# Moving twenty modulation tiles into the attention of a one-core diffusion step, with its cached keys, biases and rope prepared earlier

## The reference, cut to what matters

```python
def adaln(cond, w, b):
    m = jax.nn.silu(cond) @ w + b                 # w: 2048 x 12288, one for each of the two layers
    return [t[:, None, :] for t in jnp.split(m, 6, axis=-1)]

def att_mixer_lat(h, w_in, w_out, sink, rpb, ak, av, bk, bv):
    qa, ka, va, qb, kb, vb = att_project(h, w_in)  # w_in: 2048 x 4608
    qb, kb = rope_2d(qb), rope_2d(kb)
    oa = neighbourhood_attention(qa, ka, va, ak, av, rpb)        # 8 heads, bias rpb, cached keys ak
    ob = window_attention(qb, kb, vb, bk, bv, sink)              # 8 query heads, 2 key heads, cached keys bk
    return jnp.concatenate([oa, ob], axis=-1) @ w_out            # w_out: 2048 x 2048
```

## Time and profile before

| what | value |
|---|---|
| median of 3 runs | 2515.88 us (2503.49 to 2517.59) |
| the profiled execution's own time | 2511.74 us, its span 2509.9 us |
| TensorE busy | 2355.8 us, 94% of the span |
| VectorE, ScalarE busy | 1485.8 us (59%), 1106.8 us (44%) |
| DMA | 593.13 MB, 236 GB/s over the span |
| mean granted TensorE clock | 0.975 |

### The profile page before, as it was taken

The page is one execution under the profiler, slowest core; times in us unless marked ns, Lnnn a source line. Parts: engine busy times, 40 slices in busy tenths (PEclk is TensorE's granted clock), DMA queues, the critical chain, the costliest instruction groups (busy, mean ns, idle before and its releaser), DMA issues.

```text
span 2509.9 us, 29857 instructions
## 1 busy us (share of the span) xinstructions
PE 2355.8 (94%) x12307; PEld 1837.7 (73%) x12307; DVE 1485.8 (59%) x2049; ACT 1106.8 (44%) x1529; POOL 83.9 (3%) x139
## 2 busy tenths in 40 slices
PE   5999968879999999999997999898999999999996
PEld 3766666558888887877776777666888888778775
DVE  3464663255545455766766768764656556666665
ACT  2332242233333334555553358733444444555553
POOL 1000000000000000000000001000000000000000
PEclk9999989989999999999998999998999999999998
DMA  8898926966777777676674877777455655766763
GB/s 296 303 322 312 333 101 216 337 219 210 251 251 250 246 251 260 219 256 220 204 253 170 303 274 250 260 268 256 152 186 186 199 185 184 257 218 220 243 224 110
DMA packets 296407, 593.13 MB, mean 236 GB/s; under 512 B 11568, under 2 KB 11824, under 8 KB 296016
## 3 DMA queue, kind: packets, MB, share of 16 engines
q1 hardware_dynamic: 289744, 574.77, 66.0%
q0 software_dynamic: 6528, 16.46, 2.0%
HBM read 587.76 MB, written 3.42 MB: 236 GB/s over the span
## 4 chain that ended last, share of the span: by engine, by line
PE 82%; DMA 7%; DVE 6%; ACT 3%; issue 1%; POOL 0%; SPq 0%; DVEq 0%; ACTq 0%; POOLq 0%
PE bank L583 22%; PE bank L573 14%; PE bank L575 13%; PE bank L574 13%; PE bank L585 11%; PE bank L541 5%; DMA raw<-in_w_att_in 3%; DVE w_lo L1103 2%; DMA raw<-in_w_att_out 2%; DMA raw<-in_w_rec_in 1%; PE bank L689 1%; ACT w_hi L827 1%; PE bank L600 1%; DMA raw<-in_w_ada 1%; PE bank L558 1%
## 5 line engine op out<-in xcount | busy, mean ns | idle before, releaser
L1103 DVE TENSOR_TENSOR w_lo<-raw,w_hi 128x1024 fp32r<-128x1024 f32 x712 | 857.6, 1221 | 553.4 <-ACT w_hi L827 551.6
L827 ACT ACTIVATE w_hi<-raw 128x1024 fp32r<-128x1024 f32 x712 | 733.5, 1050 | 730.3 <-PE bank L585 189.6
L583 PE MATMUL bank<-xt,w_hi 128*128 128x512 f32 x2560 | 906.8, 399 | 4.0 <-DVE w_lo L1103 2.6
L585 PE MATMUL bank<-xt,w_lo 128*128 128x256 f32 x2560 | 712.8, 278 | 0.0
L573 PE MATMUL bank<-w_hi,xt 128*128 128x512 f32 x1568 | 628.9, 401 | 44.3 <-DVE w_lo L1103 30.2
L574 PE MATMUL bank<-w_lo,xt 128*128 128x512 f32 x1568 | 616.4, 393 | 0.0
L575 PE MATMUL bank<-w_hi,xt 128*128 128x512 f32 x1568 | 616.0, 393 | 0.0
L583 PEld LDWEIGHTS bank<-xt,w_hi 128*128 128x128 f32 x2560 | 480.3, 188 | 157.8 <-issue 33.5
L585 PEld LDWEIGHTS bank<-xt,w_lo 128*128 128x128 f32 x2560 | 481.7, 188 | 0.4
L573 PEld LDWEIGHTS bank<-w_hi,xt 128*128 128x128 f32 x1568 | 297.9, 190 | 185.1 <-DVE w_lo L1103 63.3
L575 PEld LDWEIGHTS bank<-w_hi,xt 128*128 128x128 f32 x1568 | 297.6, 190 | 64.5
(11 more groups left out here) (180 smaller groups left out, 928.4 us busy)
## 6 DMA issues: line engine op xcount, KB each, us to landing
raw<-in_w_ff SPq DMA_DIRECT2D x256, 1024.0 KB, 5.5
raw<-in_w_ada SPq DMA_DIRECT2D x192, 1024.0 KB, 7.4
raw<-in_w_att_in SPq DMA_DIRECT2D x36, 1024.0 KB, 6.1
raw<-in_w_rec_in SPq DMA_DIRECT2D x32, 1024.0 KB, 7.8
raw<-in_w_att_out SPq DMA_DIRECT2D x16, 1024.0 KB, 7.1
raw<-in_w_rec_out SPq DMA_DIRECT2D x16, 1024.0 KB, 7.4
gain_rows<-in_g_post_mix POOLq DMA_DIRECT2D x8, 256.0 KB, 6.2
gain_rows<-in_g_post_ffn POOLq DMA_DIRECT2D x8, 256.0 KB, 4.6
```

The costliest lines, as they stand in the source:

```text
L583: nc.tensor.matmul(ps[m][:, :], w_hi[:, h, k, m * P:(m + 1) * P], xt[:, c, :], start=(begin and k == 0), stop=False)
L585: mm = nc.tensor.matmul(ps[m][:, 0:NG * T], w_lo[:, h, k, m * P:(m + 1) * P], xt[:, c, 0:NG * T], start=False, stop=(end and k == 1))
L827: nc.scalar.activation(w_hi[:, n % NSPLIT, :, :], raw[:, T4.p % NRAW, 2 * q:2 * q + 2, :], ACT.Copy)\
L1103: V.tensor_tensor(w_lo[:, n % NSPLIT, :, :], raw[:, T4.p % NRAW, 2 * q:2 * q + 2, :], w_hi[:, n % NSPLIT, :, :].bitcast(fp32), ALU.subtrac ...
```

## The change

Four A tiles leave the last quarter of the projection, and the order of `att_out` becomes two M tiles, twenty A tiles, one M, twelve pairs AM and one M (before: fourteen times MAA and two M). Eighteen of the twenty A tiles stand between the parts of the attention in TensorE's order, two around the last turn of the probabilities. The blocks of modulation that end there (12 to 15, `ATT_ADA`) use bank 4 for their small products too, and the next block's first tile waits for the store. In exchange the cached keys are turned, the biases flipped and windowed, and the rope applied during the last quarter (`att_prepare`, `copy_ctx_k`, `add_window`, `rope`), for which the projection's blocks are taken in the order 6, 7, 8, 0, 2, 4, 1, 3, 5. Both bias loads move to the start of POOL's queue, behind the loads of the second modulation block. VectorE splits the second M tile of `att_out` right after the copies of step 0 (before: its halves stood after the `att_max` of step 0 and in step 2).

```diff
+ATT_ADA = (12, 13, 14, 15)
...
-    ("att_in_3", "att_in", "MAAMAAMAMAAMAMAAMAMAM"),
-    ("att_out", "att_out", "MAA" * 14 + "MM"),
+    ("att_in_3", "att_in", "MAMAMAAMAMAAMAMMM"),
+    ("att_out", "att_out", "MM" + "A" * 20 + "M" + "AM" * 12 + "M"),
...
-        Sweep("att_in", "token", w["att_in"], 0, 9, 4, "qkv", deep=True),
+        Sweep("att_in", "token", w["att_in"], 0, 9, 4, "qkv", order=(6, 7, 8, 0, 2, 4, 1, 3, 5)),
...
-            load_rpb(0)
             ada_loads(0)
             rsqrt(1)
             ada_loads(1)
+            load_rpb(0)
+            load_rpb(1)
             ada_loads_of("att_in_0")
...
-            pool.wait_ge(bias_used, 1)
-            load_rpb(1)
             ada_loads_of("att_out")
...
-                if T4.a == 0 and T4.b > 0:
+                if T4.a == 0 and T4.b - 1 in ATT_ADA:
+                    pe.wait_ge(ada_fin, T4.b)
+                elif T4.a == 0 and T4.b > 0:
                     pe.wait_ge(ada_row, T4.b)
...
+                        ada_tile(att_tiles[18])
+                        att_turn_probs(3)
+                        ada_tile(att_tiles[19])
                         att_values(3)
...
+                        if name == "att_in_3":
+                            pe.wait_ge(ctx_copied, 2)
+                            pe.wait_ge(bias_ready, 2)
                         ada_end(b)
...
+                    if name == "att_in_3" and T4.at < 3:
+                        att_prepare(T4.at)
...
+            def turn_ctx_k(bank, h0, n):
+                for j in range(n):
+                    mm = nc.tensor.transpose(ps[bank][:, j * T:(j + 1) * T], ctx_k[:, h0 + j, :], ident[:, :])
+                return mm
+            def turn_bias(bank, quad):
+                return nc.tensor.matmul(ps[bank][:, :], flip[:, :], biases[quad][:, :, :], start=True, stop=True)
+            def att_prepare(step):
+                if step == 0:
+                    pe.wait_ge(ada_fin, ada_index(0, 9) + 1)
+                    pe.wait_ge(mod_ready, KC // 2)
+                    pe.wait_ge(cache_landed, 16 * 4)
+                    turn_ctx_k(6, 0, 4)
+                    turn_ctx_k(7, 4, 4).then_inc(ctx_turned, 1)
+                elif step == 1:
+                    pe.wait_ge(ctx_copied, 1)
+                    pe.wait_ge(const_landed, 16 * 5)
+                    pe.wait_ge(rpb_landed, 16 * 8)
+                    turn_ctx_k(6, NA, NKV)
+                    turn_bias(7, 0).then_inc(ctx_turned, 1)
+                else:
+                    pe.wait_ge(ctx_copied, 2)
+                    turn_bias(6, 1).then_inc(ctx_turned, 1)
...
-                if i in (1, 2):
-                    pe.wait_ge(bias_used, i)
...
-                    mm = nc.tensor.transpose(ps[4][:, j * T:(j + 1) * T], ctx_k[:, h0 + j, :], ident[:, :])
...
-                    mm = nc.tensor.matmul(ps[4][:, :], flip[:, :], rpb[:, :, :], start=True, stop=True)
...
+            att_tiles = [T4 for T4 in SEC["att_out"] if T4.kind == "A"]
+            ada_tile(att_tiles[0])
+            ada_tile(att_tiles[1])
             att_turn(0)
+            ada_tile(att_tiles[2])
+            ada_tile(att_tiles[3])
             att_scores(0)
+            ada_end(ATT_ADA[0])
+            att_turn(1)
+            ada_tile(att_tiles[4])
+            ada_tile(att_tiles[5])
+            att_scores(1)
+            ada_tile(att_tiles[6])
+            ada_tile(att_tiles[7])
             for i in range(3):
-                att_turn(i + 1)
-                att_scores(i + 1)
+                att_turn_probs(i)
+                ada_end(ATT_ADA[i + 1])
                 att_values(i)
+                n = 4 * (i + 2)
+                ada_tile(att_tiles[n])
+                ada_tile(att_tiles[n + 1])
+                if i < 2:
+                    att_turn(i + 2)
+                    ada_tile(att_tiles[n + 2])
+                    att_scores(i + 2)
+                    ada_tile(att_tiles[n + 3])
             section("att_out")
...
+                        if q == 1 and name == "att_in_3" and T4.at in (1, 2):
+                            copy_ctx_k(T4.at - 1)
...
+                        if q == 1 and name == "att_in_3" and T4.at in (2, 3):
+                            add_window(T4.at - 2)
+                        if q == 1 and name == "att_in_3" and 4 <= T4.at < 7:
+                            rope(T4.at - 4)
...
             att_copy_qk(0)
-            rope()
+            split_early("att_out", 2, 4)
+            ada_rows_out(ATT_ADA[0])
             att_max(0)
             att_copy_qk(1)
-            split_early("att_out", 2, 3)
+            ada_store(ATT_ADA[0])
             att_norm(0)
             for i in range(4):
+                if i < 3:
+                    ada_rows_out(ATT_ADA[i + 1])
                 att_copy_probs(i)
                 if i < 3:
+                    ada_store(ATT_ADA[i + 1])
                     att_max(i + 1)
                 att_heads(i)
                 if i < 2:
                     att_copy_qk(i + 2)
-                if i == 2:
-                    split_early("att_out", 3, 4)
                 if i < 3:
                     att_norm(i + 1)
```

More of the change, by code:

```diff
@@ L49, with __init__ @@
 class Sweep:
-    def __init__(self, name, mode, weight, col0, n, tiles, out, deep=False):
-        self.name, self.mode, self.weight, self.col0, self.n, self.tiles, self.out, self.deep = \
-            name, mode, weight, col0, n, tiles, out, deep
+    def __init__(self, name, mode, weight, col0, n, tiles, out, order=None):
+        self.name, self.mode, self.weight, self.col0, self.n, self.tiles, self.out, self.order = \
+            name, mode, weight, col0, n, tiles, out, order
+        self.deep = order is not None
         self.sums = 0
@@ L63, in __init__ @@
         self.kind, self.p = kind, p
-        self.s, self.blk, self.t, self.m, self.sum = (of.get(k) for k in ("s", "blk", "t", "m", "sum"))
+        self.s, self.at, self.t, self.m, self.sum = (of.get(k) for k in ("s", "at", "t", "m", "sum"))
         self.b, self.a = of.get("b"), of.get("a")
         if kind == "M":
+            self.blk = self.s.order[self.at] if self.s.deep else self.at
             self.begin = self.s.deep or self.t == 0
@@ L120, in plan @@
                 s.sums += 1
-                blk, t = (k % s.n, k // s.n) if s.deep else divmod(k, s.tiles)
-                T4 = Tile4("M", len(seq), s=s, blk=blk, t=t, m=m, sum=token if s.mode == "token" else feature)
+                at, t = (k % s.n, k // s.n) if s.deep else divmod(k, s.tiles)
+                T4 = Tile4("M", len(seq), s=s, at=at, t=t, m=m, sum=token if s.mode == "token" else feature)
                 tiles.append(T4)
@@ L358, in hybrid_step @@
         for T4 in SEQ:
-            if T4.kind == "A" and T4.a == TILE - 1 and T4.b >= 2:
+            if T4.kind == "A" and T4.a == TILE - 1 and T4.b >= 2 and T4.b not in ATT_ADA:
                 after = [x.m for x in SEQ[T4.p:] if x.kind == "M"]
@@ L556, in ada_end @@
                 if ADA[b][2] == "cols":
+                    to = ps[4 if b in ATT_ADA else 5]
                     for m in range(BLK // P):
[L558 removed]
+                        mm = nc.tensor.matmul(to[:, NG * m:NG * m + NG], ada_sum[:, m * P:(m + 1) * P],
                                               sel_half, start=True, stop=True)
@@ L976, in norm, with copy_ctx_k @@
                                          h_mod[:, j % 2].rearrange("p c g t -> p c (g t)"), ACT.Copy).then_inc(mod_hi, 1)
+            def copy_ctx_k(step):
+                act.wait_ge(ctx_turned, step + 1)
+                if step == 0:
+                    for k in range(2):
+                        e = nc.scalar.activation(ctx_k[:, 4 * k:4 * k + 4, :],
+                                                 ps[6 + k][:, :].rearrange("p (h t) -> p h t", h=4), ACT.Copy)
+                else:
+                    e = nc.scalar.activation(ctx_k[:, NA:NA + NKV, :],
+                                             ps[6][:, 0:NKV * T].rearrange("p (h t) -> p h t", h=NKV), ACT.Copy)
+                e.then_inc(ctx_copied, 1)
             def att_copy_qk(i):
@@ L1217, in section @@
                         ada_rows_out(ADA_AT[m])
-                    if m - 1 in ADA_AT and m - 1 not in stored_after:
+                    if m - 1 in ADA_AT:
                         ada_store(ADA_AT[m - 1])
@@ new lines, in rope @@
+            def rope(n):
+                c0, c1 = ((QB0, QB0 + BLK), (QB0 + BLK, KB0), (KB0, VB0))[n]
+                dve.wait_ge(out_read_dve, DVE_READS[ms[m0("att_in_3") + n].sum] + NG)
+                h = (c1 - c0) // HD
+                qk = qkv[:, 1, c0:c1].rearrange("p (h a f) -> p h a f", h=h, a=2)
+                x1, x2 = qk[:, :, :, 0:32], qk[:, :, :, 32:64]
+                cos = rope_cos[:, :].rearrange("p (a f) -> p a f", a=2).unsqueeze(1).broadcast_to([P, h, 2, 32])
+                sin = rope_sin[:, :].rearrange("p (a f) -> p a f", a=2).unsqueeze(1).broadcast_to([P, h, 2, 32])
```

(7 more changed lines are left out.)

72 lines of the change are left out of this document (29 added, 43 removed).

## The result

The changed kernel takes 2473.72 us (median of 4 runs, 2473.0 to 2478.02) against 2515.5 us of the kernel before on the same chip (2503.49 to 2517.59): a ratio of 0.9849, 95% interval 0.9828 to 0.987. The forecast was 2480 us, with 2467 to 2500 as its range. The profiled execution took 2473.0 us, its span is 2470.9 us.

What follows compares the result with a forecast made beforehand. TensorE was taken to bound both projections, and attention's chain of copies, maxima and exponentials the part between, with weights late only behind attention. -3 + 4.7 - 35 + 0.5 = -33 us gave 2480 us, range 2467 to 2500.

Steps and rivals of the forecast that it cites:

- Attention, +4.7: Attention steps: first M tile of the output projection starts at t=69.7 instead of 65.0, including a 9 us wait.
- 5.3 us to land in an idle queue: Attention, fourth A tile: a transfer into an idle queue takes 5.3 us, so it lands at t=13.8.
- Output projection, -35: Attention's output projection: 150.3 us before, 115 us after, bounds -29 and -37.
- The breakdown of the -35: Output projection: 16 A tiles are 15 us, three block ends 2.6, the stalls 15.8.
- Last quarter, -3: Last quarter of the projection: four A tiles leave, transposes, bias flips and rope come in; -3 us, bounds -6 and +3.
- Start, +0.5 with bounds of 2.5: Kernel start: bias loads leave the first 10 us and twice as much comes later; +0.5 us, bounds -2.5 and +2.5.
- The clock didn't stay low in the steps: Rival, attention steps: clock stays low, scores take 5.4 us instead of 2.9; +8 to +10 us, 2489, chance 0.17.
- The rule on oscillation: Attention: bursts between DMA waits each start cold; speaks against the change at the fourth A tile's wait and scores 0.
- The output projection didn't keep its stalls: Rival, output projection: stalls stay because each M tile waits for its two halves; 15 us back, 2495, chance 0.12.
- tiles would only move work: Rival, attention: 18 tiles and four block ends add 20 us to the chain beside the 9 us wait; 2503, chance 0.08.
- The dry ring: Rival, attention steps: each of ten places with A tiles waits 5.3 us; 53 us more, 2526, chance 0.04.
- The better case, 2468: Case, attention: both clock and cover hold from scores 0 on; 2468 us, chance 0.04.

Runs made afterwards that it cites:

- the one with the load moved: Kernel before with only the first position-bias load moved behind the first two blocks' modulation rows: 2511.58 us, ratio 0.9986.
- the preparation alone: Changed kernel with all 32 modulation tiles back in attention's output projection and none between the steps: 2520.95 us, ratio 1.0037.
- both: Changed kernel with the second weight tile split ahead of step 0's copies and the fourth modulation tile behind scores 0 and turn 1: 2466.28 us.

## Why the prediction was right

By its steps, t counted from the end of the projection as there.

**Attention, +4.7, measured +5.6 (0.56 of the difference is the cut at 65.0).** The order of events came as forecast: A3 landed at t=13.4 (13.8), TensorE stood 8.7 us (9); scores 1 started at 27.2 (27.5), values 0 ended at 38.0 (37.9), scores 2 started at 43.3 (43.5), scores 3 at 58.5 (58.4), the first main tile at 70.0 (69.7). Only inside one piece it went otherwise: A3 itself took the half clock (1.94 us instead of 0.96) and scores 0 less of it (3.92 instead of 4.7), with nearly the same sum (5.9 and 5.7). The single number that carried this, 5.3 us to land in an idle queue, was right because the stores had landed before the tile was issued; the experiments show it at 7.8 and 9.1 when they hadn't.

**Output projection, -35, measured -38.7.** The stalls went to 0.5 us. 0.56 us of the difference are the cut of before at 387.39 and not 386.83. The rest is that 112.2 us were left where I had 115. No main tile ran at the lower clock, for which I had allowed 1 us. Another 1 us is a miscount: the recurrent projection's window holds fourteen A tiles, not thirteen, so that none had to be added for the fourteen here. The last turn and values took 4.2 us and not 4.8. The term came out a little beyond its far bound (-37). The breakdown of the -35 was wrong in two parts that nearly cancel: fourteen tiles leave the stage and not sixteen (13.4 us, not 15), and the 5.9 us that go with the clock don't stand in it.

**Last quarter, -3, measured -1.6.** Its parts came out unlike: rope cost nothing (0.5 allowed), but of the 2.9 us of waits 2.4 stayed. The waits of PE from 250.86 to 316 us:

```profile
PE bank L585 <- DVE w_lo L1180: 2.2, 3, 1.6
PE bank L574 <- DVE ada_rows L1246: 0.2, 1, 0.2
```

In this pair of profiles the term came out 1.4 us short by that, but the pair is not typical of it. In the three profiles of before and the one with the load moved the last quarter takes 66.8 to 68.2 us, 67.3 on the mean; in the ten with the new one 64.3 to 65.2, of which the first is the longest, 64.6 on the mean. The difference of the means is -2.7, close to the forecast, and the waits for late halves are 1.2 to 1.8 us in five of the others. VectorE's 18 rope instructions lie at 283.8 to 301.7 us beside matmuls. The wait of 1.6 us ends at 298.0, while the rope ahead of it had ended at 294.2; the tile of that half landed only at 295.6, 7.1 us after its issue.

**Start, +0.5 with bounds of 2.5, measured -4.8 between the two profiles.** This is the one term outside its bounds, and the repeats put its systematic part near -1, inside them. My fault was to have no bound for the scatter of the start, which is larger than the term.

**Sum.** Without the start, 5.6 - 38.7 - 1.6 + 0.4 for the rest = -34.3 us, where -33.3 was forecast; with it -39, the difference of the spans (2470.9 - 2509.95). So the mechanism carried the forecast, and 5.3 of the 6 us between -39 and the forecast -33 stand at the start, where they are mostly scatter. The two medians differ by 41.8; against the later runs of before (2511.67, 2513.64 and 2512.39 us as medians of 9, 13 and 7) the changed kernel lies 38 to 40 lower.

**Rivals.** The clock didn't stay low in the steps: from 343.7 us on it didn't fall at all, and without the tiles it fell in each of steps 1 to 3, which shows both halves of that argument. The rule on oscillation that the prediction set against the change (the Trainium skill, "TensorE: Matmul & The Clock Gate", HAM oscillation) is what happens at the single long wait of the changed kernel, where the clock fell to 0.50; in the kernel with the preparation alone the bursts start cold too, 5.07 and 5.49 us for its scores, but there the waits are for other engines and not for DMA. The output projection didn't keep its stalls. That tiles would only move work was excluded by "both": against the preparation alone, eighteen tiles and four block ends cost 61.3 - 57.2 = 4.1 us of attention there, for some 21 us of work. The dry ring appeared at A3 alone. The better case, 2468, lies inside the stated range too, so that the range left out 0.12 and not 0.15.

## What to carry to other kernels

Work that depends on nothing nearby pays most in the pauses of a latency-bound stage: it costs a fraction of its own time there, keeps the clock for the stage's own matmuls, and the stage that it is taken from gets shorter by more than the work itself: here 38.7 us, of which 16.0 are the work, the rest waits and clock. But put the first piece that still has to be loaded behind the chain's own work, not ahead of it, because TensorE takes its instructions in order; and look at what else is on the DMA engines just then, such as stores that nobody waits for. Before a microsecond is credited to an edit, profile the old kernel twice.

## What the runs showed of the hardware

- Four matmuls of 32 columns into different column groups take the time of one: a tile of four 1.07 us, a tile of one 1.05 (128x512, float32). With only that one in each tile between the steps the granted clock still stayed at 1.00 through scores 2 and 3 (350.8 to 383.3 us).
- A 1024 KB load that lands in 5.2 us without them took 7.8 and 9.1 us beside 1280 KB of stores of another queue.
- The start of an identical program is not identical: three profiles of the kernel before reach the last quarter at 251.4, 254.2 and 255.7 us, and nine kernels with the same first three quarters between 250.9 and 257.1.
